# Walking the two halves of a 512-column projection interleaved, in runs of 2 to 128 elements

## The reference, cut to what matters

```
h = x @ diff_w_in[j]             # (256, 2048) @ (2048, 5120)
q = h[..., :1536]                # 12 heads x 2 x 64
k = h[..., 1536:3072]            # 12 heads x 2 x 64
v = h[..., 3072:4608]            # 12 heads x 128
q_mem = h[..., 4608:]            # 4 memory heads x 128
```

## Time and profile before

| | |
|---|---|
| time, median of 3 runs | 2235.58 us (2231.49 to 2241.29) |
| profiled execution, span from the first to the last instruction | 2227.3 us |
| profiled execution's own time outside the span | the profile does not state it |
| TensorE matmul busy | 2175.5 us, 98% |
| VectorE busy | 1438.8 us, 65% |
| ScalarE busy | 1183.7 us, 53% |
| granted TensorE clock, mean | 0.992 |
| data moved | 406.64 MB, mean 183 GB/s |
| projection of layer 1, chunks 1 to 7 | 1105.26 to 1297.41 us, 192.15 us |

### The profile page before, as it was taken

The page is one execution under the profiler, slowest core; times in us unless marked ns, Lnnn a source line. Parts: engine busy times, 40 slices in busy tenths (PEclk is TensorE's granted clock), DMA queues, the critical chain, the costliest instruction groups (busy, mean ns, idle before and its releaser), DMA issues.

```text
span 2227.3 us, 39293 instructions
## 1 busy us (share of the span) xinstructions
PE 2175.5 (98%) x14338; PEld 1971.0 (88%) x14338; DVE 1438.8 (65%) x2434; ACT 1183.7 (53%) x2112; POOL 98.5 (4%) x91
## 2 busy tenths in 40 slices
PE   8999999999999999999999999989999999999996
PEld 8999878999999998888777777889999999988885
DVE  5657668666766675555776557587767676665555
ACT  4555455555555554444555555465555555554442
POOL 2000004000000000000130000022000000000001
PEclk9999999999999999999999999999999999999998
DMA  8554556555555555455554454556555555565552
GB/s 294 173 187 157 188 170 206 175 186 188 188 188 188 184 183 187 167 186 188 184 174 151 151 189 138 186 159 199 188 188 186 184 184 184 167 245 188 188 189 94
DMA packets 202620, 406.64 MB, mean 183 GB/s; under 512 B 7136, under 2 KB 9336, under 8 KB 202032
## 3 DMA queue, kind: packets, MB, share of 16 engines
q1 hardware_dynamic: 199248, 394.55, 52.5%
q0 software_dynamic: 3296, 11.06, 2.2%
HBM read 402.44 MB, written 3.15 MB: 182 GB/s over the span
## 4 chain that ended last, share of the span: by engine, by line
PE 92%; DVE 5%; ACT 1%; issue 1%; DMA 0%; DVEq 0%; SPq 0%; ACTq 0%
PE acc L1283 30%; PE acc L1284 30%; PE acc L1285 30%; DVE w_lo L766 3%; PE acc L1343 1%; PE acc L1520 0%; ACT w_hi L424 0%; DVE conv L914 0%; PE acc L1494 0%; PE acc L1408 0%; PE acc L1524 0%; DVE x_tok L1255 0%; PE acc L1563 0%; DVE stats L830 0%; DVE x_tok L829 0%
## 5 line engine op out<-in xcount | busy, mean ns | idle before, releaser
L766 DVE TENSOR_TENSOR w_lo<-raw,w_hi 128x512 fp32r<-128x512 f32 x1484 | 1047.0, 715 | 720.8 <-ACT w_hi L424 711.0
L424 ACT ACTIVATE w_hi<-raw 128x512 fp32r<-128x512 f32 x1480 | 927.6, 631 | 973.5 <-PE acc L1285 964.1
L1283 PE MATMUL acc<-ffn_xT,w_hi 128*128 128x256 f32 x3072 | 865.5, 282 | 9.1 <-DVE w_lo L766 8.7
L1284 PE MATMUL acc<-ffn_xT,w_hi 128*128 128x256 f32 x3072 | 861.1, 280 | 0.0
L1285 PE MATMUL acc<-ffn_xT,w_lo 128*128 128x256 f32 x3072 | 861.1, 280 | 0.0
L1283 PEld LDWEIGHTS acc<-ffn_xT,w_hi 128*128 128x128 f32 x3072 | 579.3, 189 | 12.2 <-DVE w_lo L766 10.8
L1284 PEld LDWEIGHTS acc<-ffn_xT,w_hi 128*128 128x128 f32 x3072 | 579.4, 189 | 0.2
L1285 PEld LDWEIGHTS acc<-ffn_xT,w_lo 128*128 128x128 f32 x3072 | 579.1, 189 | 0.0
L1283 PE MATMUL acc<-w_hi,ffn_act 128*128 128x512 f32 x704 | 279.2, 397 | 0.0
L1284 PE MATMUL acc<-w_lo,ffn_act 128*128 128x512 f32 x704 | 278.4, 395 | 0.0
L1285 PE MATMUL acc<-w_hi,ffn_act 128*128 128x512 f32 x704 | 276.7, 393 | 0.0
(11 more groups left out here) (196 smaller groups left out, 1129.2 us busy)
## 6 DMA issues: line engine op xcount, KB each, us to landing
raw<-in_ffn_w_up SPq DMA_DIRECT2D x176, 1024.0 KB, 5.1
raw<-in_ffn_w_down SPq DMA_DIRECT2D x88, 1024.0 KB, 5.1
raw<-in_diff_w_in SPq DMA_DIRECT2D x40, 1024.0 KB, 5.1
raw<-in_w_out SPq DMA_DIRECT2D x32, 1024.0 KB, 5.1
raw<-in_pool_w_in SPq DMA_DIRECT2D x16, 1024.0 KB, 5.2
raw<-in_mem_w_kv SPq DMA_DIRECT2D x15, 1024.0 KB, 7.2
gb<-in_ln_g POOLq DMA_DIRECT2D x12, 256.0 KB, 4.4
gb<-in_ln_b POOLq DMA_DIRECT2D x12, 256.0 KB, 6.1
```

The costliest lines, as they stand in the source:

```text
L424: nc.scalar.activation(w_hi[:, j, 0:st.width], raw[:, k % SLOTS, j * CHUNK:j * CHUNK + st.width], ACT.Copy).then_inc(hi_made, 1)
L766: nc.vector.tensor_tensor(w_lo[:, j, 0:st.width], raw[:, k % SLOTS, j * CHUNK:j * CHUNK + st.width], w_hi[:, j, 0:st.width].bitcast(F32), ...
L1283: pe.matmul(out, w[0], x[0], start=start, stop=False, skip_group_check=True)
L1284: pe.matmul(out, w[0], x[1], start=False, stop=False, skip_group_check=True)
```

## The change

A table gives the chunks with index 1 to 7 a run length of 2, 4, 8, 16, 32, 64 and 128; the chunks 0, 8 and 9 have none. These are seven chunks by the table. For a run length n, `folded` views the 512 contiguous elements as two halves of 256 and walks them as n elements of the first half, n of the second, the next n of the first, and so on. The same view is put on the moving operand (`w_hi` and `w_lo`) and on the output in PSUM, so that each product still lands in its own column. The stationary operand is as it was, and so are the number of matmuls, their columns, and all that other engines do.

```diff
+READ_RUNS = (None, 2, 4, 8, 16, 32, 64, 128, None, None)

-        def tokens_granule(st, c, k, j, src, bank0, piece=None):
+        def folded(ap, run):
+
+            return ap if run is None else ap.rearrange("p (h g n) -> p g h n", h=2, n=run)
+
+        def tokens_granule(st, c, k, j, src, bank0, piece=None, run=None):
...
-                ins = product3(bank(bank0 + t, 0, CHUNK), (src[:, kt, 0, ts], src[:, kt, 1, ts]),
-                               (w_hi[:, j, :], w_lo[:, j, :]), (k, j) == (0, 0), (k, j) == (st.pieces - 1, PIECE - 1))
+                ins = product3(folded(bank(bank0 + t, 0, CHUNK), run), (src[:, kt, 0, ts], src[:, kt, 1, ts]),
+                               (folded(w_hi[:, j, :], run), folded(w_lo[:, j, :], run)), (k, j) == (0, 0), (k, j) == (st.pieces - 1, PIECE - 1))
...
-                        tokens_granule(s_diff, c, k, j, xT, 2 * (c % 2), OUT_PIECES[1][k] if c == DIFF_LAST else None)
+                        tokens_granule(s_diff, c, k, j, xT, 2 * (c % 2), OUT_PIECES[1][k] if c == DIFF_LAST else None,
+                                       READ_RUNS[c])
```

## The result

The changed kernel takes 2245.52 us (median of 6 runs, 2242.76 to 2253.38), the kernel before 2235.12 us beside it: a ratio of 1.0055, 95% interval [1.0033, 1.0077]. It is some 10 to 12 us slower, where the forecast was no change (2236 us) with a range to 2262.

A forecast was written before the change was run, and what follows sets the result against it. TensorE was taken as the only bound; 672 matmuls x 0 ns added 0 us to the 2227.3 us span, and the 8.3 us between span and median was carried over: 2236 us, range 2226 to 2262.

The forecast's parts named there:

- What bounds the kernel: Whole kernel: TensorE, busy 98% of the span, is the only bound; a longer matmul moves the end by as much.
- I take 0 ns per jump: Main step, chunks 1 to 7: the interleaved walk costs nothing, 672 x 0 = 0 us, as VectorE's rotary rows suggest.
- The bounds: All 672 matmuls: at most +132 us at plain float32 pace, at least -13.4 us if 20 ns each were saved.
- The sign that I had set for a wrong main step: Chunk 1, n = 2: a distance between matmul starts above 350 ns would show the main step wrong.
- Rival B: Chunk 1 alone stalls at n = 2: 430 ns a matmul, +18.9 us less 0.5 of wait, 2254 us; chance 0.20.
- Rival C: Chunks 1 to 7: every jump costs a cycle, 0.417 ns, halving from chunk to chunk; +20.3 us, 2254 us; chance 0.12.
- Every pair of neighbours stays together: Chunks 1 to 7: second reason for 0 ns per jump, held to be true at n = 2 too.
- The reading that I had put beside rival B: SBUF lines: if TensorE takes float32r in pairs, a run of 2 has one hit per visit and fails alone.
- Rival D: Chunks 1 to 7: any walk not one straight run streams at plain float32 pace; +132 us, 2368 us; chance 0.07.
- F: Chunks 1 to 7: the view is folded back into one straight run; forecast's time; counted within no cost's 0.56.
- E: Chunks 1 to 7 faster: the new order avoids the 20 ns over a column a cycle; -13.4 us, 2222 us; chance 0.05.
- The other waits go too: TensorE's waits besides `w_lo`, 1.9 us in all, would vanish because slower granules leave ScalarE and VectorE more time.

## Why the prediction was right in its range and wrong in its main step

- **What bounds the kernel: right.** TensorE's matmul pace set the end, the clock stayed at 1.00, and what the matmuls lost (+12.9 us in the stretches) came out in the time.
- **"I take 0 ns per jump": the step that failed.** Measured per matmul: +104 ns at n = 2, +18 at 4, +10 at 8, +7 at 16, +4 at 32, nothing from 64 on, where the forecast had 0 in all. The row it leaned on, VectorE's rotary steps, has runs of 8 on an engine that takes 1.04 ns an element; it says nothing on how TensorE fetches. The bounds were the sound part: +132 and -13.4 us hold the +12.9. The sign that I had set for a wrong main step, above 350 ns at n = 2, did not show at 337, so it was set too high. That the time stayed within half a percent or so of no change is luck of the table, in which 96 of 672 matmuls have the costly run; with pairs in six chunks the kernel took 125 us more. The range held because it was drawn to take in B and C.
- **"Every pair of neighbours stays together" as a reason for 0: wrong for the operand, right for PSUM.** The unit on the reading side is the aligned group of 4, not the pair. The Trainium skill's wish for two hits on a 16-byte line ("Advanced Engine Details and Errata", "SBUF Cachelines") is met by a run of 2, if a hit is counted per element, and does not protect it: 337 to 487 ns. The reading that I had put beside rival B, that a visit must use more than one pair, fits the runs, but for the two neighbouring groups (218 ns).
- **Rival B (0.20), the shortest run alone: nearest.** It named the chunk, and its 430 ns are near what four places and more take (436 to 487), though that is chance, for it was borrowed from the pace of the plain float32 stream; with the change's two places it is 337, and chunks 2 to 5 are not free.
- **Rival C (0.12), a cycle per jump: a coincidence.** 104 ns / 256 jumps is 0.41 ns, just its price, and 340 ns was its mark for chunk 1. Chunk 2 should then have shown +53 ns and showed +18; pairs in four places cost twice as much for the same jumps, and 128 jumps of 8 elements cost none. A mark that one number can meet did not tell the rivals apart; the seven stretches and the table of distances did.
- **Rival D and the Trainium skill's broad sentence: fallen,** chunk 7 is untouched. **F: fallen,** the pace moved. **E** is alive in another place: some 17 of the 20 ns over a column a cycle go with how the operand is fetched, but the change's walk does not save them.
- **"The other waits go too": wrong.** The `w_lo` wait went, the one for `diff_probs` grew by 1.0 us, because the shift changed which VectorE steps meet GpSimd's; the waits of the earlier trace rows are 2.6 us in all, where they were 2.4.
- **The sum by what was measured:** (104 + 18 + 10 + 7 + 4) x 96 ns = 13.7 us for the walk, and 1.0 for `diff_probs`; the seven stretches show 12.9, so some 1.8 us were taken up, 0.5 of them by the `w_lo` wait of chunk 1.

Still open: why the pace of runs of 4 goes 226, 248, 277, 268, 251 ns for jumps of 16 to 256 elements, and why pairs in two places cost half of what they cost in four. No run here shows what lies behind either. A run of one element was not tried.

## What to carry to other kernels

Where TensorE is the bound, the moving operand's walk is a cost of its own: keep runs to whole, aligned groups of 16 bytes, and don't cut float32 operands into pairs (up to twice the time); runs of one whole group can still cost up to 44 ns in 233, by the distance of the jump, and longer runs cost less. The PSUM side was free in every walk measured here, with runs of 2 to 128 float32, so a permutation belongs there. And the straight walk isn't the floor: measure from start to start, compare with a column a cycle, and if there is a gap try the order of fetching; here runs of 4 with 64-byte steps gave 2.2% of the whole kernel for three lines.

## What the runs showed of the hardware that I had not expected

- A float32r stream of 512 columns takes 233 ns straight, 226 to 231 with 64-byte steps, and 216 when each group is used at least twice in a row, all at a granted clock of 1.00.
- Runs of 4 that begin 8 bytes off the 16-byte groups, counted from the operand's first element, take 331 ns where aligned ones take 245.
- Of the jumps tried, the dearest for runs of 4 is 64 elements (256 bytes), 277 ns; at 256 elements it is 251 again.
